# One more FFN pair by seven block products, with GpSimd taking part of the sums of x

## The chip, the cores and the metric

The kernel runs on one core of a Trainium2 chip. The metric is the device time of one execution in microseconds (us), the median of several runs. TensorE (PE in the profile) multiplies; VectorE (DVE), ScalarE (ACT) and GpSimd (POOL) work on tiles in SBUF; SyncE (SP) issues most DMAs and GpSimd some.

## The reference

One inference step of a 4-layer decoder for 512 prompt tokens and 8 sample tokens (520 columns), model width 1024, in float32. Each layer has a mixer (pooling, convolution, differential attention, pooling) and then an FFN, and it is the FFN that the change touches:

```python
def swiglu(h, w_gate, w_up, w_down):
    return (jax.nn.silu(h @ w_gate) * (h @ w_up)) @ w_down
...
    xp = xp + swiglu(rmsnorm(xp, norm_ffn[i]), ffn_w_gate[i], ffn_w_up[i], ffn_w_down[i])
```

D_FF is 2816, that is 22 tiles of 128 rows for gate and 22 for up.

## The kernel before

Activations lie transposed: 8 tiles of 128 channels by 520 tokens, taken by TensorE in two halves of 260. Every float32 value is split into a high part and a low part (ScalarE writes the high part, rounded to fp32r; VectorE subtracts it from the value and writes the low part), and each product is made of three matmuls: high by high, high by low, low by high.

A gate tile and its up tile are a **pair**; an FFN has 22. An **ordinary pair** is two **units** of 8 x 2 x 3 = 48 matmuls, 96 in all: `unit` on the un-normed x, and `rstd` multiplies the result (`gate_n`, `up2`). `h2` is up2 by silu2. Four pairs of a layer are ordinary (PLAIN = 4): units 0 to 7. The other 18 are **pairs in sevens**: gate and up tile by two halves of the channels form a 2 by 2 product with the two halves of the tokens, done in seven block products (Winograd's form of Strassen) of 4 x 3 = 12 matmuls, 84 in all. They run in `seven_blocks` on TensorE and `join` on ScalarE and VectorE; b counts the blocks 0 to 6.

The sevens need x otherwise than the units do. VectorE makes the normed halves xn0 and xn1 (16 `scaled` instructions of 260 columns, in the first ordinary pair), then four sums of them, `xt[:, 0]`, `xt[:, 1]`, `xt3` and `xt[:, 2]` (1040 columns each), and for each block b the high part (ScalarE, `x_high(b)`, into `xn_hi`, `xt_hi`, `late_hi`) and the low part (VectorE, `x_low(b)`). They are placed by hand between the instructions of the ordinary pairs; c counts these. Weights of a pair in sevens need sums too: two on VectorE (`w_sum_2`, `w_sum_4`) and two by accumulating DMAs that GpSimd issues (`weight_sums`); the second of them adds to a half of w_up that SyncE loads into `w_sum` after a wait for the sums of x.

Each engine runs its own program in order, and semaphores tie them. The ones of the change are `x_scaled`, `x_summed`, `xs_hi_ok`, `xs_lo_ok`. TensorE's `unit` n waits for `split_lo` (VectorE's low part of the weights, `w_lo`), block b for `blk_lo` and `xs_lo_ok`; blocks 2, 4 and 6 add to what block 0 left in PSUM, and wait until ScalarE has copied it (`copy_begun`, tile `begun`, semaphore `begun_ok`).

## Time and profile before

| | |
|---|---|
| median of 3 runs | 2039.98 us (2039.18 to 2043.82) |
| the profiled execution | 2047.97 us, its span 2046.2 us |
| busy share of the span | TensorE 98%, VectorE 66%, ScalarE 52%, GpSimd 19% |
| granted TensorE clock, mean | 0.991 |
| layer 0's ordinary pairs | 53.5 to 101.5 us |

The profile is one execution. Its times are from the span's start. In a timeline a row gives start, duration, engine, line, operation, output from inputs with shapes, and in brackets how long the engine was idle ahead of it and who ended that.

### The profile page before, as it was taken

The numbers are of one execution on the slowest core, as the hardware profiler recorded it, in microseconds if no ns is written. First come the engines' busy times: TensorE is split into PE (matmuls) and PEld (weight loads), VectorE is DVE, ScalarE is ACT, GpSimd is POOL, SyncE is SP. The second block draws the span as 40 slices with busy tenths as digits, with TensorE's granted clock in tenths as the row PEclk, the third lists the DMA queues.
The fourth block names the chain that finished last, engine by engine and source line by source line (L and its number), as shares of the span: only waits on it lengthen the run. The fifth ranks groups of instructions, "written<-read, shape, count | busy, mean of one in ns | idle before, by whom it ended". The sixth has DMA issues, their size and how long they took to land.

```text
span 2046.2 us, 41692 instructions
## 1 busy us (share of the span) xinstructions
PE 2006.8 (98%) x16576; PEld 1941.2 (95%) x16576; DVE 1345.7 (66%) x2268; ACT 1061.5 (52%) x1842; POOL 380.8 (19%) x397
## 2 busy tenths in 40 slices
PE   8999999999899999999999979999999999999999
PEld 7999999998599999999999859999999999999998
DVE  4994586468768945864466655885587368936852
ACT  4563465365455634653777753463365355624642
POOL 3210110169421101101111114110111120101101
PEclk8999999999999999999999999999999999999999
DMA  5363664244214636643432252363564314636642
GB/s 188 106 181 91 163 182 128 81 126 115 78 63 113 182 93 165 181 129 88 175 112 88 86 194 92 113 175 97 150 187 138 109 57 127 172 93 182 180 118 80
DMA packets 99526, 264.86 MB, mean 129 GB/s; under 512 B 13353, under 2 KB 16329, under 8 KB 99316
## 3 DMA queue, kind: packets, MB, share of 16 engines
q1 hardware_dynamic: 74756, 217.14, 32.9%
q0 software_dynamic: 24208, 44.72, 11.9%
q8 instruction: 121, 1.98, 0.4%
q10 hardware_dynamic: 384, 0.55, 0.1%
q14 instruction: 57, 0.47, 0.1%
HBM read 213.40 MB, written 8.60 MB: 108 GB/s over the span
## 4 chain that ended last, share of the span: by engine, by line
PE 87%; POOL 4%; DVE 4%; ACT 2%; issue 1%; DMA 1%; SPq 0%; ACTq 0%; POOLq 0%; DVEq 0%
PE acc L693 44%; PE pair L893 20%; PE acc L893 10%; PE bank L893 5%; POOL conv L2600 4%; PE pair L1095 1%; PE pair L774 1%; PE bank L1115 1%; DMA hist_rows<-in_state_pool 1%; DVE w_lo L1858 1%; PE pair L1070 1%; DVE xn L1999 1%; DVE xt L2066 0%; ACT w_hi L1328 0%; PE bank L1105 0%
## 5 line engine op out<-in xcount | busy, mean ns | idle before, releaser
L1328 ACT ACTIVATE w_hi<-raw 128x768 fp32r<-128x768 f32 (+1 forms) x220 | 199.3, 906 | 429.9 <-PE acc L693 427.6
L693 PE MATMUL acc<-h_hi,w_hi 128*128 128x260 f32 x1408 | 399.5, 284 | 0.0
L693 PE MATMUL acc<-h_lo,w_hi 128*128 128x260 f32 x1408 | 398.3, 283 | 0.0
L693 PE MATMUL acc<-h_hi,w_lo 128*128 128x260 f32 x1408 | 397.6, 282 | 0.0
L1858 DVE TENSOR_TENSOR w_lo<-raw,w_hi 128x768 fp32r<-128x768 f32 (+1 forms) x220 | 240.9, 1095 | 216.4 <-ACT w_hi L1328 211.0
L693 PE MATMUL acc<-xin_hi,w_hi 128*128 128x260 f32 x1152 | 332.6, 289 | 6.0 <-DVE w_lo L1858 4.8
L693 PE MATMUL acc<-xin_hi,w_lo 128*128 128x260 f32 x1152 | 326.2, 283 | 0.0
L693 PE MATMUL acc<-xin_lo,w_hi 128*128 128x260 f32 x1152 | 325.6, 283 | 0.0
L693 PEld LDWEIGHTS acc<-h_hi,w_hi 128*128 128x128 f32 x1408 | 265.2, 188 | 0.6
L693 PEld LDWEIGHTS acc<-h_hi,w_lo 128*128 128x128 f32 x1408 | 265.1, 188 | 0.0
L693 PEld LDWEIGHTS acc<-h_lo,w_hi 128*128 128x128 f32 x1408 | 264.8, 188 | 0.0
L693 PEld LDWEIGHTS acc<-xin_hi,w_hi 128*128 128x128 f32 x1152 | 217.5, 189 | 20.5 <-issue 13.9
L2537 POOL DMA_DIRECT2D raw<-raw x72 | 62.1, 862 | 922.4 <-DMA raw<-in_ffn_w_up 922.4
L693 PEld LDWEIGHTS acc<-xin_lo,w_hi 128*128 128x128 f32 x1152 | 217.6, 189 | 0.2
L693 PEld LDWEIGHTS acc<-xin_hi,w_lo 128*128 128x128 f32 x1152 | 217.5, 189 | 0.0
L1489 ACT ACTIVATE begun<-pair 128x260 f32<-128x260 f32 x216 | 83.7, 388 | 174.5 <-PE pair L893 174.3
L2034 DVE TENSOR_TENSOR block<-raw,block 128x512 fp32r<-128x512 f32 x140 | 95.7, 686 | 52.7 <-ACT block L1475 52.7
L893 PE MATMUL pair<-xn_hi,block 128*128 128x260 f32 x576 | 114.8, 281 | 0.0
L2503 POOL TENSOR_TENSOR sqacc<-sqacc,sq 128x520 f32<-128x520 f32 x48 | 75.5, 1574 | 208.4 <-ACT sq L1334 207.9
L893 PE MATMUL pair<-xt_hi,block 128*128 128x260 f32 x544 | 109.5, 284 | 0.0
L893 PE MATMUL bank<-xn_hi,block 128*128 128x260 f32 x544 | 109.2, 282 | 0.0
L1475 ACT ACTIVATE w_hi<-w_sum 128x512 fp32r<-128x512 f32 x144 | 90.2, 627 | 29.9 <-PE acc L893 12.9
(442 smaller groups left out, 5377.8 us busy)
## 6 DMA issues: line engine op xcount, KB each, us to landing
raw<-in_ffn_w_gate SPq DMA_DIRECT2D x88, 512.0 KB, 3.6
raw<-in_ffn_w_up SPq DMA_DIRECT2D x88, 512.0 KB, 4.5
raw<-in_ffn_w_down SPq DMA_DIRECT2D x64, 384.0 KB, 3.2
raw<-in_ffn_w_down SPq DMA_DIRECT2D x64, 320.0 KB, 2.9
w_sum<-in_ffn_w_up SPq DMA_DIRECT2D x72, 256.0 KB, 4.8
raw<-raw POOLq DMA_DIRECT2D x72, 256.0 KB, 3.4
w_sum<-raw POOLq DMA_DIRECT2D x72, 256.0 KB, 4.1
raw<-in_attn_w_qkv SPq DMA_DIRECT2D x24, 512.0 KB, 3.6
```

The lines of the kernel that those rows point to most:

```text
L693: last = pe.matmul(acc[:, b, 0:HALF], w[:, w_tile * P:(w_tile + 1) * P], v[:, h * HALF:(h + 1) * HALF], start=start and t == 0, stop=stop ...
L774: last = pe.matmul(pair[:, m % 2, b * P:(b + 1) * P], x_tok[:, b, cols], band_s[:, b, g, 0:P], start=True, stop=b == 0)
L893: last = pe.matmul(block_bank(J, b), w[:, cols], v[:, k, :], start=k + t == 0 and b in (0, 1, 3, 5), stop=k == 3 and t == 2, skip_group_ch ...
L1070: last = pe.matmul(pair[:, t, 0:HALF], blk, sq[:, 0, t * HALF:(t + 1) * HALF], start=True, stop=True)
L1328: act.activation(w_hi[n.slot(2)][:, 0:cols], raw[:, q.slot(4), 0:cols], ACT.Copy).then_inc(split_hi, 1)
L1475: act.activation(block_w(j, b)[0], block_of(b, q, J), ACT.Copy).then_inc(blk_hi, 1)
L1489: act.activation(begun[b // 2][:], pair[:, J % 2, 0:HALF], ACT.Copy).then_inc(begun_ok, 1)
L1858: dve.tensor_tensor(w_lo[n.slot(2)][:, 0:cols], raw[:, raw_of(n).slot(4), 0:cols], w_hi[n.slot(2)][:, 0:cols].bitcast(F32), ALU.subtract). ...
L2034: dve.tensor_tensor(lo, block_of(b, raw_of_pair(layer, j), PAIRS * layer + j), hi.bitcast(F32), ALU.subtract).then_inc(blk_lo, 1)
L2503: pool_e.tensor_tensor(sqacc[:], sqacc[:], sq[:, m % 2, :], ALU.add).then_inc(sq_added, 1)
L2537: pool_e.dma_start(up[:, 0:512], up[:, 512:1024], accum_op=ALU.add).then_inc(ups_ok[J % 2], 16)
L2600: pool_e.tensor_tensor(out, out, prod_p[:, p % 3, :], ALU.add).then_inc(prod_added, 1)
```

## The change

PLAIN goes from 4 to 3: each layer has three ordinary pairs (units 0 to 5) and nineteen in sevens. So the work on x has to be placed in three pairs. Two sums (`xt[:, 2]`, `xt3`) and the low parts of blocks 4 and 6 go from VectorE to GpSimd, with a semaphore `x_by_pool`. VectorE's remaining work on x stands in two places of the second ordinary pair: two sums and the low part of block 0 ahead of up2, the low parts of blocks 1 to 3 at its end; that of block 5 stays in the last.

```diff
-PLAIN = 4
+PLAIN = 3
...
-                            sp.wait_ge(x_summed, 4 * layer + 4)
+                            sp.wait_ge(x_summed, 2 * layer + 2)
...
-                    pe.wait_ge(xs_lo_ok, 7 * layer + b + 1)
+                    if b in XP_LOW:
+                        pe.wait_ge(x_by_pool, 4 * layer + XP_LOW[b])
+                    else:
+                        pe.wait_ge(xs_lo_ok, 5 * layer + min(b, 4) + 1)
...
                     if c == 1:
                         dve.wait_ge(x_scaled, layer + 1)
                         dve.wait_ge(stored, 16 * STORED[("pool0", "conv", "attn", "pool1")[layer]])
-                        for to, a, b, made in ((xt[:, 0], xn1[:, 0:4], xn0[:, 0:4], 0), (xt[:, 1], xn1[:, 4:8], xt[:, 0], 1),
-                                         (xt3[:], xn0[:, 4:8], xt[:, 1], 2), (xt[:, 2], xn1[:, 0:4], xn1[:, 4:8], 0)):
...
-                    if c + 2 == PLAIN:
-                        x_low(1)
-                        x_low(2)
+                        x_sum(0)
+                        x_sum(1)
+                        x_low(0)
...
                     if c + 1 == PLAIN:
                         low(0, 4)
-                        x_low(4)
-                        for b in (5, 6):
-                            x_low(b)
-                            low(0, b)
+                        x_low(5)
+                        low(0, 5)
+                        low(0, 6)
...
-                    if c + 3 == PLAIN:
-                        x_low(0)
                     if c + 2 == PLAIN:
-                        x_low(3)
+                        for b in range(1, 4):
+                            x_low(b)
...
+            def sums(layer):
+
+                pool_e.wait_ge(x_scaled, layer + 1)
+                pool_e.tensor_tensor(xt[:, 2], xn1[:, 0:4], xn1[:, 4:8], ALU.subtract).then_inc(x_by_pool, 1)
+                up_sum(layer, 0)
+                pool_e.wait_ge(x_summed, 2 * layer + 2)
+                pool_e.tensor_tensor(xt3[:], xn0[:, 4:8], xt[:, 1], ALU.subtract).then_inc(x_by_pool, 1)
+                crossed_sum(layer, 0)
+                up_sum(layer, 1)
+                crossed_sum(layer, 1)
+                x_low(layer, 4)
+                x_low(layer, 6)
+                for j in range(2, PAIRS):
+                    up_sum(layer, j)
+                    crossed_sum(layer, j)
```

ScalarE's code is the same but for its waits, and since its places are counted from PLAIN it moves too. In layer 0 ScalarE's rows from the first ordinary pair's second weight split on were, before:

```order
L1328 ACTIVATE w_hi1_58<-raw_56 128x1024
L1480 ACTIVATE h_hi_77<-h2_102 128x520
L1328 ACTIVATE w_hi0_57<-raw_56 128x1024
L1499 ACTIVATE silu2_99<-gate_n_100 128x520
L1328 ACTIVATE w_hi1_58<-raw_56 128x1024
L1480 ACTIVATE h_hi_77<-h2_102 128x520
L1460 ACTIVATE xn0_hi_80<-xn0_79 128x1040
```

and in the change:

```order
L1335 ACTIVATE w_hi1_58<-raw_56 128x1024
L1489 ACTIVATE h_hi_77<-h2_102 128x520
L1469 ACTIVATE xn0_hi_80<-xn0_79 128x1040
L1335 ACTIVATE w_hi0_57<-raw_56 128x1024
L1508 ACTIVATE silu2_99<-gate_n_100 128x520
L1469 ACTIVATE xn0_hi_80<-xn0_79 128x1040
L1469 ACTIVATE xt_hi_82<-xt_81 128x1040
L1335 ACTIVATE w_hi1_58<-raw_56 128x1024
```

The high part of block 0's x (`x_high(0)`, the first xn0_hi) moved from the end of the second ordinary pair to the end of the first, ahead of the split for unit 4 (w_hi0). VectorE's rows of layer 0 from the second ordinary pair's gate_n on were, before:

```order
L2050 TENSOR_TENSOR gate_n_100<-acc,rstd_52 128x520
L1858 TENSOR_TENSOR w_lo0_59<-raw_56,w_hi0_57 128x1024
L2066 TENSOR_TENSOR xt_81<-xn1_88,xn0_79 128x1040
L2066 TENSOR_TENSOR xt_81<-xn1_88,xt_81 128x1040
L2066 TENSOR_TENSOR xt3_89<-xn0_79,xt_81 128x1040
L2066 TENSOR_TENSOR xt_81<-xn1_88 128x1040
L2071 TENSOR_TENSOR up2_101<-acc,rstd_52 128x520
L2080 TENSOR_TENSOR h2_102<-up2_101,silu2_99 128x520
L1858 TENSOR_TENSOR w_lo1_60<-raw_56,w_hi1_58 128x1024
L2040 TENSOR_TENSOR h_lo_78<-h2_102,h_hi_77 128x520
```

and in the change:

```order
L2068 TENSOR_TENSOR gate_n_100<-acc,rstd_52 128x520
L1867 TENSOR_TENSOR w_lo0_59<-raw_56,w_hi0_57 128x1024
L2015 TENSOR_TENSOR xt_81<-xn1_88,xn0_79 128x1040
L2015 TENSOR_TENSOR xt_81<-xn1_88,xt_81 128x1040
L2029 SCALAR_TENSOR_TENSOR xn0_lo_84<-xn0_79,xn0_hi_80 128x1040
L2084 TENSOR_TENSOR up2_101<-acc,rstd_52 128x520
L2092 TENSOR_TENSOR h2_102<-up2_101,silu2_99 128x520
L1867 TENSOR_TENSOR w_lo1_60<-raw_56,w_hi1_58 128x1024
L2058 TENSOR_TENSOR h_lo_78<-h2_102,h_hi_77 128x520
L2027 TENSOR_TENSOR xn0_lo_84<-xn0_79,xn0_hi_80 128x1040
L2027 TENSOR_TENSOR xt_lo_85<-xt_81,xt_hi_82 128x1040 x2
L2038 TENSOR_TENSOR w_sum_94<-raw_56 128x512
```

Two of the four sums left this place and block 0's low part came ahead of up2; three low parts follow h_lo, where an ordinary pair's gate_n stood before. GpSimd's queue in layer 0, which held only the accumulating DMAs here, begins in the change with

```order
L2565 TENSOR_TENSOR xt_81<-xn1_88 128x1040
L2547 DMA raw_56<-raw_56 128x512
L2568 TENSOR_TENSOR xt3_89<-xn0_79,xt_81 128x1040
L2554 DMA w_sum_94<-raw_56 128x512
L2547 DMA raw_56<-raw_56 128x512
L2554 DMA w_sum_94<-raw_56 128x512
L2560 TENSOR_TENSOR xt_lo_85<-xt_81,xt_hi_82 128x1040
L2560 TENSOR_TENSOR late_lo_91<-xt3_89,late_hi_90 128x1040
```

Four computing instructions of 1040 columns stand among the DMAs of the first two pairs in sevens.

## Rows read from the trace of the kernel before

**Rows 1.** The page, part 1: busy time, share of the span, instructions of each engine.
```profile
PE 2006.8 (98%) x16576; PEld 1941.2 (95%) x16576; DVE 1345.7 (66%) x2268; ACT 1061.5 (52%) x1842; POOL 380.8 (19%) x397
```
**Rows 2.** The chain in order of time, layer 0: start, duration, what.
```profile
110.33 2.88 PE pair L893 x24
120.40 2.88 PE pair L893 x24
```
**Rows 3.** Timeline of TensorE, layer 0: the first matmul of unit 5.
```profile
84.16 0.39 PE L693 MATMUL acc<-xin_hi,w_hi 128*128 128x260 f32 x1 [0.78 <-DVE w_lo L1858]
```
**Rows 4.** Timeline of ScalarE, layer 1: weight splits released by a unit's end.
```profile
634.51 1.06 ACT L1328 ACTIVATE w_hi<-raw 128x1024 fp32r<-128x1024 f32 x1 [3.54 <-PE acc L693]
640.25 1.06 ACT L1328 ACTIVATE w_hi<-raw 128x1024 fp32r<-128x1024 f32 x1 [3.73 <-PE acc L693]
```
**Rows 5.** Windows: stretch, length; busy us (count) of PE, PEld, DVE, ACT, POOL; clock, DMA.
```profile
53.50:101.70 48.20, 47.39 (x390) 47.00 (x391) 43.95 (x57) 26.81 (x34) 8.40 (x9) 1.00 0.41 112
```
**Rows 6.** Timeline of VectorE, layer 0.
```profile
71.67 3.29 DVE L1999 SCALAR_TENSOR_TENSOR xn<-x,vec,rstd 128x260 f32<-128x260 f32 x8
74.88 0.69 DVE L2050 TENSOR_TENSOR gate_n<-acc,rstd 128x520 f32<-128x520 f32 x1
...
76.62 1.23 DVE L2066 TENSOR_TENSOR xt<-xn,xn 128x1040 f32<-128x1040 f32 x1
...
94.80 0.68 DVE L2020 TENSOR_TENSOR w_sum<-raw 128x512 f32<-128x512 f32 x1
...
96.74 0.68 DVE L2034 TENSOR_TENSOR block<-raw,block 128x512 fp32r<-128x512 f32 x1
```
**Rows 7.** Timeline of ScalarE, layer 0.
```profile
72.01 1.06 ACT L1328 ACTIVATE w_hi<-raw 128x1024 fp32r<-128x1024 f32 x1 [1.32 <-PE acc L693]
...
83.55 1.06 ACT L1460 ACTIVATE xn_hi<-xn 128x1040 fp32r<-128x1040 f32 x1
84.51 1.05 ACT L1328 ACTIVATE w_hi<-raw 128x1024 fp32r<-128x1024 f32 x1
...
96.85 0.64 ACT L1499 ACTIVATE silu<-gate_n 128x520 f32<-128x520 f32 x1 [0.70 <-DVE gate_n L2050]
97.40 0.61 ACT L1475 ACTIVATE w_hi<-raw 128x512 fp32r<-128x512 f32 x1
...
103.15 0.39 ACT L1489 ACTIVATE begun<-pair 128x260 f32<-128x260 f32 x1 [0.37 <-PE pair L893]
```
**Rows 8.** Timeline of VectorE, layer 1.
```profile
635.15 0.69 DVE L2050 TENSOR_TENSOR gate_n<-acc,rstd 128x520 f32<-128x520 f32 x1
```
**Rows 9.** Timelines of VectorE and GpSimd, layer 1; last row from pooling, undisturbed.
```profile
611.42 1.23 DVE L1858 TENSOR_TENSOR w_lo<-raw,w_hi 128x1024 fp32r<-128x1024 f32 x1 [0.39 <-ACT w_hi L1328]
612.57 1.80 DVE L1870 SCALAR_TENSOR_TENSOR xin_lo<-x,vec,xin_hi 128x520 fp32r<-128x520 f32 x1
...
612.00 1.81 POOL L2503 TENSOR_TENSOR sqacc<-sqacc,sq 128x520 f32<-128x520 f32 x1 [3.91 <-ACT sq L1334]
...
1669.30 0.76 DVE L1870 SCALAR_TENSOR_TENSOR xin_lo<-x,vec,xin_hi 128x520 fp32r<-128x520 f32 x1
```
**Rows 10.** The same two engines in the first pooling layer.
```profile
50.71 3.21 POOL L2503 TENSOR_TENSOR sqacc<-sqacc,sq 128x520 f32<-128x520 f32 x2 [2.40 <-ACT sq L1334]
...
52.69 1.41 DVE L1891 SCALAR_TENSOR_TENSOR x<-acc,vec,x 128x520 f32<-128x520 f32 x2
```
**Rows 11.** GpSimd's instructions by line: durations in ns, lowest/median/highest.
```profile
L2654 POOL TENSOR_TENSOR o_tok<-o_tok,o_tmp x8: 1042/1047/1047, 1222.0 to 1231.2; 128x512 f32<-128x512 f32 x8
L2581 POOL TENSOR_TENSOR diag_z<-const,taps_z x4: 1967/1982/2436, 478.4 to 515.7; 128x1024 f32<-128x1024 f32 x4
L2600 POOL TENSOR_TENSOR conv<-conv,prod_p x60: 1261/1296/2284, 428.3 to 535.7; 128x512 f32<-128x512 f32 x60
```
**Rows 12.** The page, part 6: DMA issues, KB each, us from issue to landing.
```profile
w_sum<-in_ffn_w_up SPq DMA_DIRECT2D x72, 256.0 KB, 4.8
...
w_sum<-raw POOLq DMA_DIRECT2D x72, 256.0 KB, 4.1
```

More of the change, by code:

```diff
@@ L480, in trunk_step @@
         xs_hi_ok, xs_lo_ok = sem("xs_hi_ok"), sem("xs_lo_ok")
+        x_by_pool = sem("x_by_pool")
         begun_ok, joined, new_scaled = sem("begun_ok"), sem("joined"), sem("new_scaled")
@@ L1457, in x_high @@
                     if X_SUMMED[b]:
-                        act.wait_ge(x_summed, 4 * layer + X_SUMMED[b])
+                        act.wait_ge(x_summed, 2 * layer + X_SUMMED[b])
+                    if XP_SUMMED[b]:
+                        act.wait_ge(x_by_pool, 4 * layer + XP_SUMMED[b])
                     own, hi, _ = XS[b]
@@ L2000, in scaled, with x_sum @@
                     return last
+                def x_sum(t):
+                    if t:
+                        dve.wait_ge(x_summed, 2 * layer + 1)
+                    dve.tensor_tensor(xt[:, t], xn1[:, 4 * t:4 * t + 4], xt[:, 0] if t else xn0[:, 0:4], ALU.subtract)\
+                       .then_inc(x_summed, 1)
                 def x_low(b):
@@ L2005, in x_low @@
                     if X_READ[b]:
-                        dve.wait_ge(x_summed, 4 * layer + X_READ[b])
+                        dve.wait_ge(x_summed, 2 * layer + X_READ[b])
+                    if XP_READ[b]:
+                        dve.wait_ge(x_by_pool, 4 * layer + XP_READ[b])
                     own, hi, lo = XS[b]
@@ L2529, in store_stage, with up_sum @@
                 pool_e.dma_start(states_s, stage[hist:hist + DEC, :]).then_inc(stored, 16)
-            def weight_sums(layer):
-                for j in range(PAIRS):
-                    q, J = raw_of_pair(layer, j), PAIRS * layer + j
-                    gate, up = raw[:, q.slot(4), :], raw[:, (q + 1).slot(4), :]
-                    pool_e.wait_ge(landed[(q + 1).slot(4)], ((q + 1).turn(4).v + 1) * 16)
-                    pool_e.dma_start(up[:, 0:512], up[:, 512:1024], accum_op=ALU.add).then_inc(ups_ok[J % 2], 16)
-                    pool_e.wait_ge(landed[q.slot(4)], (q.turn(4).v + 1) * 16)
-                    pool_e.wait_ge(crossed_in[J % 2], 16 * (J // 2 + 1))
-                    pool_e.dma_start(crossed(J), gate[:, 0:512], accum_op=ALU.add).then_inc(crossed_ok[J % 2], 16)
+            def up_sum(layer, j):
+                q, J = raw_of_pair(layer, j), PAIRS * layer + j
+                up = raw[:, (q + 1).slot(4), :]
+                pool_e.wait_ge(landed[(q + 1).slot(4)], ((q + 1).turn(4).v + 1) * 16)
+                pool_e.dma_start(up[:, 0:512], up[:, 512:1024], accum_op=ALU.add).then_inc(ups_ok[J % 2], 16)
@@ new lines, in crossed_sum, with x_low @@
+            def crossed_sum(layer, j):
+                q, J = raw_of_pair(layer, j), PAIRS * layer + j
+                pool_e.wait_ge(landed[q.slot(4)], (q.turn(4).v + 1) * 16)
+                pool_e.wait_ge(crossed_in[J % 2], 16 * (J // 2 + 1))
+                pool_e.dma_start(crossed(J), raw[:, q.slot(4), 0:512], accum_op=ALU.add).then_inc(crossed_ok[J % 2], 16)
+            def x_low(layer, b):
+                pool_e.wait_ge(xs_hi_ok, 7 * layer + b + 1)
+                own, hi, lo = XS[b]
+                pool_e.tensor_tensor(lo, own, hi.bitcast(F32), ALU.subtract).then_inc(x_by_pool, 1)
@@ L2573, in _ @@
                     state_rows(0)
-                weight_sums(3 * q)
+                sums(3 * q)
                 if q:
@@ L2608, in _ @@
                 add_squares(3)
-                weight_sums(1)
+                sums(1)
                 add_squares(4)
@@ L2661, in _ @@
                 add_squares(5)
-                weight_sums(2)
+                sums(2)
                 add_squares(6)
```

10 lines of the change are left out of this document (5 added, 5 removed).

## The prediction, written before the changed kernel was run

> **What bounds the kernel now.** The page's first part comes first: TensorE is busy 98% of the span, VectorE 66%, GpSimd 19% [rows 1]. The chain of work in order of time then shows what an FFN costs. Pieces of one block repeat every 10.07 us, one period per pair in sevens [rows 2], and a pair has 7 blocks of 12 matmuls, so a matmul costs 10.07 / 84 = 0.12 us. An ordinary pair is two units of 48; ScalarE's splits, each released by the end of a unit, stand 5.74 us apart [rows 4], again 0.12 us a matmul. So TensorE is never late in an FFN, except once each in layers 0 and 3, before unit 5 (of units 0 to 7): its last matmul of unit 4 ended 0.78 us before 84.16 [rows 3]; a matmul's record ends 0.28 after its start, so unit 5 was due at 84.16 - 0.78 - 0.28 + 0.12 = 83.2, and with a slow second matmul the wait costs about 1.0 us. Unit 4 began at 83.2 - 5.74 = 77.5. Whatever takes matmuls away there is worth their time; whatever makes TensorE wait costs the wait in full.
>
> What limits the ordinary pairs is how full VectorE is. In layer 0 it is busy 43.95 of the 48.2 us before the first block [rows 5]. The timeline of VectorE shows it back to back: each instruction starts about 0.09 us before the one ahead ends [rows 6].
>
> **The change, part by part.**
>
> *Fewer matmuls.* In each layer one pair goes from 96 matmuls to 84: 12 x 0.12 = 1.44 us, four layers 5.8 us gained. That is the whole gain.
>
> *Less time for the same work on x.* Two units fewer are 11.5 us less before block 0.0 (block b of pair j is j.b). VectorE loses with them one ordinary pair's instructions, and two sums and two low parts of 1.23 us each [rows 6] that go to GpSimd. The rest must now fit. I walk layer 0 instruction by instruction, in the new order, with the durations of the rows, 0.03 us from an engine's end to another's start and 0.12 to TensorE's.
>
> *GpSimd's price.* No GpSimd instruction of before has two full inputs of 1040. The form with one spread input takes 1.05 us at 512 and 1.97 at 1024, so about 0.12 is fixed; two full inputs at 512 take 1.26 when undisturbed [rows 11], hence (1.26 - 0.12) x 1040 / 512 + 0.12 = 2.4 us. Bounds: 2.0 (the one-spread-input form) and 2.54 (twice the whole of 1.26 and a little).
>
> *GpSimd stops VectorE.* The rows at 612 us show it. GpSimd's sum starts at 612.00 while VectorE's w_lo still runs and takes 1.81 us instead of 1.26; VectorE's xin_lo, at 612.57, takes 1.80 instead of 0.76 and ends 0.56 after GpSimd's [rows 9]. Both read two tensors in SBUF. An instruction that reads PSUM and one SBUF tensor isn't stopped: two of them take 1.41 us as usual under a GpSimd pair [rows 10]. I take 2.2 of GpSimd's 2.4 us as lost when VectorE wants the path at once, since xin_lo ended 0.2 earlier than a fresh start would have. The Trainium skill ("SBUF — State Buffer", section "SBUF: two separate sides") calls the shared pair an exclusive lock held for the whole instruction. By that reading all 2.4 us are lost and the sum below is +18.6 instead of +15; the row's 0.56 us speaks for a little less.
>
> *Unit 4 (layer 0).* This is a new wait: ScalarE's first high part of x stands ahead of the split for unit 4 and waits for the last of the scaled parts, which VectorE ends at 71.67 + 3.29 = 74.96 [rows 6]. Before, that split ran at 72.01 [rows 7] and nothing waited for it. Now the high part runs from 75.0 (1.06 us, the next one 0.97 later [rows 7]), the split from 76.0 to 77.1. GpSimd started its first sum at 75.0 and ends at 77.4, so VectorE's w_lo (1.23 [rows 9]) begins effectively at 77.25, ends 78.46, and unit 4 starts at 78.6 instead of 77.5: 1.05 us.
>
> *Unit 5.* VectorE: two sums to 80.9, low part of block 0's x to 82.0, up2 from PSUM to 82.6. GpSimd, released at 80.9, waits for the low part and holds 81.95 to 84.4; h2 reads SBUF and ends at 84.9 instead of 83.4; w_lo ends at 86.0. Unit 5 is due at 84.3: 1.8 us.
>
> *Block 0.0.* Behind it VectorE has h_lo (0.7), three low parts (1.15 each from start to start), two w_sums (0.7 each), gate_n (0.6) and the low part of the block (0.7) [rows 6]: 92.6. TensorE is due at 91.9: 0.85 us.
>
> *Blocks 0.2 and 0.4.* ScalarE's silu comes after gate_n, then two w_hi (0.53 each from start to start), two high parts (0.97 each) and the copy begun [rows 7]. Before, ScalarE did the first of them while TensorE was still at the last unit; now gate_n itself is late (ends 92.0) and they stand end to end: silu 92.0, w_hi 92.6 and 93.1, high parts 93.65 and 94.6, begun 95.6 to 96.0. Block 0.2 is due at 92.7 + 2 x 1.44 = 95.6: 0.5 us. The second begun, behind two more w_hi, costs block 0.4 another 0.5.
>
> *Blocks 0.5, 0.6, 1.2.* GpSimd's low parts run 94.7 to 97.2 and 97.6 to 100.0 and stop VectorE twice, 2.0 and 2.1 us, where it has w_lo, late_lo and h2 in line. The w_lo of block 0.5 ends at 101.6 (due 101.0): 0.8; h2 at 102.8 holds ScalarE, whose third begun comes at 103.8: 0.75; the same lag reaches pair 1's block 2: 0.5. From pair 2 on the slack of the steady state has absorbed it.
>
> GpSimd's DMAs aren't on the path: the half of w_up is issued at 80.9, lands 4.8 us later, the addition another 4.1 [rows 12], at 89.8; its reader comes at 93.1. SyncE's wait for the sums falls from four to two, so the loads behind it in its queue go out no later than VectorE frees their slots. Behind GpSimd's wait for the last high part stand only pair 2's additions, whose weights land later anyway.
>
> *Sum.* Layers 0 and 3: 1.05 + 1.8 + 0.85 + 0.5 + 0.5 + 0.8 + 0.75 + 0.5 = 6.8 of waiting, less the 1.0 there now, less 1.44: +4.4 us each. In layer 1 gate_n starts at 635.15 [rows 8], and unit 3's end releases ScalarE at 640.25 [rows 4], so unit 4 is due at about 640.05, 4.9 us after gate_n; in layer 0 that is 77.5 - 74.9 = 2.6. Unit 4 then has no wait. From gate_n to unit 5's start the walk took 86.1 - 74.9 = 11.2 us: 646.35, due 645.8, 0.55 us. The rest is the same: 0.55 + 0.85 + 0.5 + 0.5 + 0.8 + 0.75 + 0.5 = 4.5, less 1.44: +3.1 each, in layer 2 too, whose rows repeat layer 1's. Together 2 x 4.4 + 2 x 3.1 = +15 us. The profiled execution of 2047.97 us (span 2046.2) would become 2063; it stands 8 us above the median, and I carry the difference over: 2039.98 + 15 = 2055 us.
>
> With GpSimd's 2.0 us the same walk gives +9; with 2.54 us and the whole of it lost, +20.5. The skill's "GPSIMD Engine Reference" ("Instruction dispatch") gives about 2.5 cycles an element for two inputs. An estimate by that figure and the 1.2 GHz of the "SBUF — State Buffer" page is 2.2 us for 1040, and the sum would be +11; no row here has this shape.
>
> **The rivals.** *VectorE isn't stopped (not slower).* If these instructions don't share the path as those at 612 us did, the same walk leaves, in layer 0, unit 4 0.9, unit 5 0.4, blocks 0.0, 0.2 and 0.4 0.85, 0.5 and 0.5: 3.15 - 1.0 - 1.44 = +0.7; in layer 1 0.86 - 1.44 = -0.6. Together +0.1: no change, 2040. For it: GpSimd is on other tensors. Against it: so it was at 612 us. It decides where a stop is short: with GpSimd instructions of 1.6 us (stops of 1.4) the walk gives +4, with 1.2 us +1, with under 0.9 us +0.1.
>
> *GpSimd is slower than its shape says.* 3.1 us an instruction, twice the disturbed 1.5: the walk gives +26, 2066. The rows at 512 that last 2.28 us [rows 11] contain waiting, which I count already.
>
> *The waits are hidden.* If ScalarE and VectorE keep up after all, the 5.8 us come in full and the two present waits may go: -6 to -8, 2033. Against it: VectorE's 43.95 busy us [rows 5] must fit into 11.5 us less, less what leaves.
>
> **How the numbers follow.** Forecast +15 (with its bounds +9 to +20.5): 0.74. A mixture, where only some of the four instructions stop VectorE, +5 to +9 (the two sums alone give +7 in the walk): 0.07. GpSimd at 3.1: 0.07. Not stopped: 0.08. Hidden: 0.04. A measurement of this kernel can tell about 0.2%, 4 us, from no change, so slower has 0.74 + 0.07 + 0.07 = 0.88, within 0.08, faster 0.04. The range takes in forecast and mixture, +5 to +20.5 and 2 us at the top for the step from profile to median: 2045 to 2063; 0.19 is left out.
>
> **What would show it.** VectorE instructions with two SBUF inputs of about 2.9 to 3.4 us instead of 0.7 to 1.2 beside GpSimd's four, two per place; GpSimd's xt at 2.4 to 3.5 us. TensorE's first wait on w_lo at unit 4 in layers 0 and 3 alone, a longer one at unit 5 in all four, then waits in pair 0 on w_lo and begun; pairs from 2 on at 10.07 us. Eight pairs in sevens before the first down stage. The walk is wrong if VectorE's instructions beside GpSimd's keep their length, if TensorE waits for GpSimd itself, or if later pairs are slower as well.

## The result, and the profile after

The changed kernel takes 2055.57 us (median of six runs, 2052.31 to 2061.46); the kernel before, timed beside it, 2041.38 us. The ratio is 1.0062 with a 95% interval of 1.0047 to 1.0077: 12.7 us slower, between 9.6 and 15.7. Forecast were 15 us.

In all comparisons below a change of time is the ratio less one, times 2041 us.

The page of the profile, part 1 (busy time, share of the span, instructions) and the first line of part 4 (shares of the chain that ended last) of the changed kernel:

```profile
PE 1999.5 (97%) x16528; PEld 1928.1 (94%) x16528; DVE 1365.3 (66%) x2292; ACT 1072.9 (52%) x1878; POOL 430.4 (21%) x421
...
PE 79%; DVE 7%; issue 4%; ACT 4%; POOL 4%; DMA 1%; ACTq 0%; SPq 0%; DVEq 0%; POOLq 0%
```

TensorE has 48 matmuls and 7.3 us less to do than in [rows 1], and a longer span. VectorE has 19.6 us *more* busy time, although four instructions a layer went to GpSimd. Two things make this up. A pair in sevens gives VectorE more to do than an ordinary pair: with all four pieces left on VectorE (the first experiment below) it is busy 1359.9 us, 14.2 more than before. And a stopped instruction counts as busy: the sixteen pieces that left are some 20 us of work (1.23 us each), and VectorE is busy 5.4 us more than in that experiment, not 20 less. GpSimd is busy 49.6 us more.

The timeline of TensorE, layer 0 (start, duration, what; idle time before it and what ended it), all the waits after the first unit:

```profile
69.60 0.38 PE L697 MATMUL acc<-xin_hi,w_hi 128*128 128x260 f32 x1 [0.99 <-DVE w_lo L1867]
...
77.17 0.39 PE L697 MATMUL acc<-xin_hi,w_hi 128*128 128x260 f32 x1 [1.55 <-DVE w_lo L1867]
...
83.77 0.39 PE L900 MATMUL pair<-xn_hi,block 128*128 128x260 f32 x1 [0.59 <-DVE block L2052]
...
87.08 0.39 PE L900 MATMUL pair<-xt_hi,early 128*128 128x260 f32 x1 [0.15 <-ACT begun L1498]
...
90.39 0.39 PE L900 MATMUL pair<-xt_hi,w_hi 128*128 128x260 f32 x1 [0.15 <-ACT begun L1498]
...
92.88 0.39 PE L900 MATMUL acc<-late_hi,w_hi 128*128 128x260 f32 x1 [0.79 <-DVE w_lo L2052]
...
95.04 0.38 PE L900 MATMUL pair<-late_hi,w_hi 128*128 128x260 f32 x1 [0.47 <-ACT begun L1498]
...
99.99 0.39 PE L900 MATMUL pair<-xt_hi,block 128*128 128x260 f32 x1 [0.37 <-ACT begun L1498]
```

In place of the one row of [rows 3] there are eight: units 4 and 5, then blocks 0.0, 0.2, 0.4, 0.5, 0.6 and 1.2, and no other. The idle times in brackets add up to 5.06 us. Each leaves out what a restart costs beside it (the prediction counted 1.0 us for a bracket of 0.78), and with 0.22 us for each of the eight the sum is 6.8.

The clean measure is the length of the stage from the first matmul of the feed-forward to the first of the down projection. Here it is for each layer, in us (read from the timeline of TensorE and the chain in order of time):

| layer | before | after | difference | forecast |
|---|---|---|---|---|
| 0 | 53.53 to 172.21: 118.68 | 44.51 to 167.90: 123.39 | +4.7 | +4.4 |
| 1 | 615.81 to 733.79: 117.98 | 611.53 to 732.95: 121.42 | +3.4 | +3.1 |
| 2 | 1288.01 to 1405.85: 117.84 | 1286.21 to 1407.60: 121.39 | +3.6 | +3.1 |
| 3 | 1680.62 to 1799.18: 118.56 | 1683.91 to 1807.24: 123.33 | +4.8 | +4.4 |

Together +16.5 us. The two profiled spans differ only by 8.3 (2054.5 and 2046.2), since the profiled execution of before came to its first feed-forward 9 us later. The windows from 20 to 36 us show why, before and then after (length; busy us and count of PE, PEld, DVE, ACT, POOL; granted clock; DMA):

```profile
20.00:36.00 16.00, 16.00 (x72) 14.92 (x71) 5.87 (x13) 3.29 (x6) 0.00 (x0) 0.51 0.47 180
20.00:36.00 16.00, 16.00 (x142) 15.96 (x141) 10.39 (x20) 8.36 (x15) 2.56 (x3) 1.00 0.50 194
```

TensorE did 72 matmuls there at a granted clock of 0.51, nearly all at 1.2 GHz, and 142 at 1.00, that is 2.4 GHz. The first feed-forward began between 44.5 and 53.8 us in the thirteen profiles of this study, whose kernels do the same up to there: by 45.8 us in the five in which the clock stayed at 1.00, after 51.6 us in the six in which it was low for over 13 us. So the stages are compared and not the spans.

Who makes TensorE wait is seen on VectorE and GpSimd, whose timelines of layer 0 go side by side:

```profile
66.00 2.46 POOL L2565 TENSOR_TENSOR xt<-xn 128x1040 f32<-128x1040 f32 x1 [10.99 <-DVE xn L2008]
...
72.06 3.36 POOL L2568 TENSOR_TENSOR xt<-xn,xt 128x1040 f32<-128x1040 f32 x1 [2.75 <-DVE xt L2015]
...
85.88 2.42 POOL L2560 TENSOR_TENSOR xt_lo<-xt,xt_hi 128x1040 fp32r<-128x1040 f32 x1 [2.79 <-ACT xt_hi L1469]
88.59 2.54 POOL L2560 TENSOR_TENSOR late_lo<-xt,late_hi 128x1040 fp32r<-128x1040 f32 x1 [0.29 <-ACT late_hi L1469]
```
```profile
68.01 1.53 DVE L1867 TENSOR_TENSOR w_lo<-raw,w_hi 128x1024 fp32r<-128x1024 f32 x1 [1.48 <-ACT w_hi L1335]
69.47 1.23 DVE L2015 TENSOR_TENSOR xt<-xn,xn 128x1040 f32<-128x1040 f32 x1
...
71.89 1.23 DVE L2029 SCALAR_TENSOR_TENSOR xn_lo<-xn,xn_hi 128x1040 fp32r<-128x1040 f32 x1
73.04 0.69 DVE L2084 TENSOR_TENSOR up<-acc,rstd 128x520 f32<-128x520 f32 x1
73.84 2.13 DVE L2092 TENSOR_TENSOR h<-up,silu 128x520 f32<-128x520 f32 x1
...
86.05 2.80 DVE L2052 TENSOR_TENSOR w_lo<-w_sum,w_hi 128x512 fp32r<-128x512 f32 x1
88.77 3.46 DVE L2027 TENSOR_TENSOR late_lo<-xn,late_hi 128x1040 fp32r<-128x1040 f32 x1
92.15 0.68 DVE L2052 TENSOR_TENSOR w_lo<-w_sum,w_hi 128x512 fp32r<-128x512 f32 x1
```

Four instructions of VectorE are long, each beside one of GpSimd: w_lo 1.53 us (1.22 elsewhere), h 2.13 (0.70), w_lo 2.80 (0.68), late_lo 3.46 (1.23). GpSimd waits too: its second sum takes 3.36 us, since VectorE's low part (71.89 to 73.12) stands in the way. The two engines take turns. The instruction at 73.04, which reads PSUM and one tensor in SBUF, keeps its 0.69 us beside GpSimd's.

### The profile page after: what moved, and what is told of

Same layout as the page of the kernel before. It is cut to its first block, busy times and chain, and to the rows that moved or that the text cites. A ratio compares the mean times of both kernels' runs of the same rounds, so it can differ in the third digit from the quotient of the medians.

```text
span 2054.5 us, 41744 instructions
## 1 busy us (share of the span) xinstructions
PE 1999.5 (97%) x16528; PEld 1928.1 (94%) x16528; DVE 1365.3 (66%) x2292; ACT 1072.9 (52%) x1878; POOL 430.4 (21%) x421
## 4 chain that ended last, share of the span: by engine, by line
PE 79%; DVE 7%; issue 4%; ACT 4%; POOL 4%; DMA 1%; ACTq 0%; SPq 0%; DVEq 0%; POOLq 0%
PE acc L697 37%; PE pair L900 20%; PE acc L900 10%; PE bank L900 5%; POOL conv L2636 4%; DVE xn L2008 1%; PE pair L1102 1%; ACT w_hi L1335 1%; DVE w_lo L1867 1%; PE bank L1122 1%; PE pair L1077 1%; DMA hist_rows<-in_state_pool 1%; DVE xt_lo L2027 0%; PE pair L778 0%; PE pair L1272 0%
## 5 line engine op out<-in xcount | busy, mean ns | idle before, releaser
L1335 ACT ACTIVATE w_hi<-raw 128x768 fp32r<-128x768 f32 (+1 forms) x212 | 190.8, 900 | 400.2 <-PE acc L697 397.7
L1867 DVE TENSOR_TENSOR w_lo<-raw,w_hi 128x768 fp32r<-128x768 f32 (+1 forms) x212 | 232.3, 1096 | 221.7 <-ACT w_hi L1335 216.2
L697 PE MATMUL acc<-xin_hi,w_hi 128*128 128x260 f32 x1024 | 296.0, 289 | 10.7 <-DVE w_lo L1867 9.5
L697 PE MATMUL acc<-xin_hi,w_lo 128*128 128x260 f32 x1024 | 289.3, 282 | 0.0
L697 PE MATMUL acc<-xin_lo,w_hi 128*128 128x260 f32 x1024 | 289.0, 282 | 0.0
L697 PEld LDWEIGHTS acc<-xin_hi,w_hi 128*128 128x128 f32 x1024 | 192.6, 188 | 26.0 <-issue 13.8
L697 PEld LDWEIGHTS acc<-xin_lo,w_hi 128*128 128x128 f32 x1024 | 192.8, 188 | 0.2
L697 PEld LDWEIGHTS acc<-xin_hi,w_lo 128*128 128x128 f32 x1024 | 192.8, 188 | 0.0
L900 PE MATMUL pair<-xn_hi,block 128*128 128x260 f32 x608 | 121.6, 282 | 2.4 <-DVE block L2052 2.4
L2052 DVE TENSOR_TENSOR w_lo<-w_sum,w_hi 128x512 fp32r<-128x512 f32 x152 | 112.6, 741 | 2.0 <-ACT w_hi L1484 1.3
```

Source lines behind the costliest of these rows:

```text
L697: last = pe.matmul(acc[:, b, 0:HALF], w[:, w_tile * P:(w_tile + 1) * P], v[:, h * HALF:(h + 1) * HALF], start=start and t == 0, stop=stop ...
L900: last = pe.matmul(block_bank(J, b), w[:, cols], v[:, k, :], start=k + t == 0 and b in (0, 1, 3, 5), stop=k == 3 and t == 2, skip_group_ch ...
L1335: act.activation(w_hi[n.slot(2)][:, 0:cols], raw[:, q.slot(4), 0:cols], ACT.Copy).then_inc(split_hi, 1)
L1867: dve.tensor_tensor(w_lo[n.slot(2)][:, 0:cols], raw[:, raw_of(n).slot(4), 0:cols], w_hi[n.slot(2)][:, 0:cols].bitcast(F32), ALU.subtract). ...
L2052: dve.tensor_tensor(lo, block_of(b, raw_of_pair(layer, j), PAIRS * layer + j), hi.bitcast(F32), ALU.subtract).then_inc(blk_lo, 1)
```

## The experiments

The theory: an instruction of GpSimd that reads two operands from SBUF stops VectorE's work on two operands in SBUF for as long as it runs, and this, with the shorter front, makes the waits. The rival: nothing is stopped, and only the number and the order of VectorE's own instructions count. Every "walk" in what follows is the prediction's hand calculation, done for another order of the same instructions with the same durations.

### All four pieces back on VectorE

```diff
-        X_SUMMED = (0, 0, 2, 1, 0, 0, 0)
-        XP_SUMMED = (0, 0, 0, 0, 1, 0, 2)
+        X_SUMMED = (0, 0, 2, 1, 4, 0, 3)
...
                         x_sum(1)
+                        x_sum(2)
+                        x_sum(3)
                         x_low(0)
...
                         low(0, 4)
-                        x_low(5)
-                        low(0, 5)
-                        low(0, 6)
+                        x_low(4)
+                        for b in (5, 6):
+                            x_low(b)
+                            low(0, b)
...
-                pool_e.wait_ge(x_scaled, layer + 1)
-                pool_e.tensor_tensor(xt[:, 2], xn1[:, 0:4], xn1[:, 4:8], ALU.subtract).then_inc(x_by_pool, 1)
...
```

> Three ordinary pairs as in the changed kernel, but all four pieces (two sums, two low parts) are back on VectorE, so that GpSimd computes nothing in these stretches. The theory under test (a GpSimd instruction of 2.4 us stops VectorE's three-operand work for 2.2 us of it) and its rival (it stops nothing, only number and place of VectorE's own instructions count) both give this kernel the same time, since there is nothing to stop: walked step by step with the durations of the traces, +10 us against the kernel before. What they differ in is whether the changed kernel (+15) lies above it. In layers 0 and 3 the walk has waits of 0.9 us in TensorE before unit 4, 2.8 before unit 5, 0.85, 0.5 and 0.55 before blocks 0.0, 0.2 and 0.4, and hardly any before blocks 0.5, 0.6 and 1.2, which in the changed kernel have 0.5 to 0.8 each. If the rival holds, this kernel is slower than the changed one (which has 4 pieces less on VectorE) by about 10 us; by the theory it is faster by about 5.

Measured: ratio 1.0065 (1.0043 to 1.0087), +13.3 us; the stages are 122.05, 120.04, 120.06 and 122.18 us long, together 11.3 more than before, where the changed kernel has 16.5. In layer 1 the bracketed waits are 1.26 before unit 5, 0.58, 0.15 and 0.15 before blocks 0.0, 0.2 and 0.4, and no row with a wait later, as walked. So with four instructions a layer *more* on VectorE the kernel isn't slower than the changed one (+13.3 against +12.7 us): the rival's 10 us on top are refuted. That it is 5 us faster is read from the stages alone; the timed runs show no difference.

Most of the loss, then, is there without GpSimd: three ordinary pairs are too short for VectorE's front in this order. Layers 0 and 3 have one more thing in them, though, that the walk didn't have. The windows of this kernel in layer 0 (columns as above):

```profile
76.00:79.00 3.00, 0.63 (x6) 0.42 (x4) 2.90 (x4) 0.98 (x2) 0.00 (x0) 1.00 0.82 244
79.00:82.00 3.00, 2.82 (x13) 2.82 (x14) 3.00 (x5) 1.66 (x3) 0.87 (x1) 0.56 0.63 126
82.00:85.00 3.00, 3.00 (x24) 3.00 (x23) 2.96 (x5) 0.64 (x1) 1.46 (x2) 0.87 0.98 253
```

After the wait of 2.55 us before unit 5 the granted clock is 0.56, then 0.87: some of the time ran at 1.2 instead of 2.4 GHz, 13 matmuls in 3 us instead of 25. While TensorE was slow VectorE caught up, and the waits before 0.0, 0.2 and 0.4 are missing in this layer. Layer 3 does the same: 0.56 in the 3 us from 1714 on, behind a wait of 2.54 us. The lengths came out near the walk's (+3.4 and +3.6, where its terms give +3.2) because one replaced the other, which the walk had not foreseen.

### Only the low parts back, only the sums back

The first has the changed kernel's sums on GpSimd and the diff above for x_low alone; the second the reverse.

> The changed kernel with its two low parts back on VectorE; the two sums stay on GpSimd. By the theory (the second pair of GpSimd instructions costs more in stopped VectorE time than it saves): the waits before blocks 0.5 and 0.6 go, that before 1.2 shrinks to 0.1, units 4 and 5 keep theirs (1.05 and 1.8 in layers 0 and 3): +7 us against the kernel before, 8 faster than the changed kernel. By the rival (nothing is stopped) it would be at +0.5, and the changed kernel at +0.1.

> The changed kernel with its two sums back on VectorE; the two low parts stay on GpSimd. By the theory: units 4 and 5 wait 0.9 and 2.8 us in layers 0 and 3, unit 5 1.4 in layers 1 and 2, blocks 0.5, 0.6 and 1.2 keep 0.5 to 0.8: +18 us against the kernel before, above the changed kernel. By the rival: +10, and the blocks 0.5 and 0.6 do not wait.

Measured: 1.0033 (1.0018 to 1.0047), +6.7 us, with the low parts back; 1.0086 (1.0059 to 1.0112), +17.6 us, with the sums back. The stages add +8.2 and +19.3 us. TensorE's timeline in layer 1 of the version with the low parts back, from unit 5 on:

```profile
647.67 0.39 PE L696 MATMUL acc<-xin_hi,w_hi 128*128 128x260 f32 x1 [0.57 <-DVE w_lo L1863]
...
654.27 0.39 PE L896 MATMUL pair<-xn_hi,block 128*128 128x260 f32 x1 [0.59 <-DVE block L2048]
...
657.58 0.39 PE L896 MATMUL pair<-xt_hi,early 128*128 128x260 f32 x1 [0.16 <-ACT begun L1494]
```

No row has a wait at 0.5, 0.6 or 1.2. In the version with the sums back it is the other way round: 1.26 us before unit 5, and 0.85, 0.42 and 0.36 before blocks 0.5, 0.6 and 1.2. So the two pairs of GpSimd instructions are separate, and have opposite signs: the sums on GpSimd save 3 us by the stages (11.3 to 8.2), since they shorten the crowded place before unit 5; the low parts on GpSimd cost 8 us (8.2 to 16.5 with the sums there, 11.3 to 19.3 without), since VectorE is stopped for 2.1 and 2.2 us to save it twice 1.15. Without them the kernel is at +6.7 instead of +12.7 us. This is the largest single part of the loss that is GpSimd's.

### Four ordinary pairs, the four pieces on GpSimd

```diff
-PLAIN = 3
+PLAIN = 4
...
-                        x_low(0)
+                    if c + 2 == PLAIN:
+                        x_low(1)
+                        x_low(2)
...
+                    if c + 3 == PLAIN:
+                        x_low(0)
                     if c + 2 == PLAIN:
-                        for b in range(1, 4):
-                            x_low(b)
+                        x_low(3)
```

> The kernel before (four ordinary pairs, VectorE's work on x in its three places), with only the four pieces moved to GpSimd at the points where the changed kernel has them. By the theory: one wait of 1.05 us before unit 4 and one of 0.6 before unit 7 in layers 0 and 3, then 0.4, 0.75 and 0.5 before blocks 0.5, 0.6 and 1.2 (0.5 before 0.6 and 1.2 in layers 1 and 2): +6.5 us against the kernel before. By the rival VectorE is only relieved: -2 us, since the kernel before's own wait before unit 5 goes too.

Measured: 1.0038 (1.0022 to 1.0055), +7.8 us, where the theory had +6.5 and the rival -2. In layer 0 the brackets are 0.97 before unit 4, 0.23, 0.43 and 0.37 before blocks 0.5, 0.6 and 1.2; that before unit 7 has no row. The stages add +7.2 us. GpSimd's help costs time also where the number of ordinary pairs stays.

### Extra work for GpSimd that nobody needs

In the kernel before, nothing is moved; GpSimd gets one of three things at each of the four points, with the result in a scratch tensor.

```diff
+            def extra():
+
+                if made[0]:
+                    pool_e.wait_ge(extra_done, made[0])
+                pool_e.tensor_tensor(sq[:].rearrange("p a b -> p (a b)"), const[:, 0:2 * T], const[:, 8:2 * T + 8], ALU.subtract).then_inc(extra_done, 1)
+                made[0] += 1
...
             def weight_sums(layer):
 
+                pool_e.wait_ge(x_scaled, layer + 1)
+                extra()
                 for j in range(PAIRS):
...
+                    if j == 0:
+                        pool_e.wait_ge(x_summed, 4 * layer + 2)
+                        extra()
...
+                    if j == 1:
+                        for b in (4, 6):
+                            pool_e.wait_ge(xs_hi_ok, 7 * layer + b + 1)
+                            extra()
```

In the second and third the subtraction is replaced by two tensor_copy (128x1040 and 128x520) and by three memset. ScalarE's squares of the next pooling, which use the same scratch, wait for it; that lies outside the stages.

> The kernel before, in which nothing of VectorE's or ScalarE's work is moved; only GpSimd gets something to do that nobody needs: one subtraction of 128x1040 (two operands read from SBUF, the result written into the scratch of squares, free at that time) at each of the four points at which the changed kernel gives it a sum or a low part. The output is the reference's. Nobody waits for these results in the front of the feed-forward, only GpSimd's own weight sums stand behind them. By the theory that a two-operand instruction of GpSimd stops VectorE: +16 us against the kernel before, by waits in layers 0 and 3 of 1.05 before unit 4, 1.6 before unit 5, 0.5, 1.9 and 0.5 before blocks 0.5, 0.6 and 1.2, and the same without unit 4 and with 0.4 before unit 5 in layers 1 and 2; VectorE's instructions beside them last 2.8 us and more where they lasted 0.7 and 1.23. By the rival (the moved pieces' own order and waits cost the time, not the use of the memory by GpSimd): within 1 us of the kernel before.

> As the run with four extra two-operand subtractions, but at each of the four points GpSimd makes two copies (one operand read, one written) of 128x1040 and 128x520. The output is the reference's. If any GpSimd instruction of that length stops VectorE, the time is as there, about +16 us; if only instructions with two operands do, it is within 1 us of the kernel before, and VectorE's instructions beside them keep their 0.7 and 1.23 us. I hold the second for likelier, since the kernel's own copies on GpSimd stand in stretches in which nothing can be read on this.

> As the run with four extra two-operand subtractions, but with three memsets (nothing read, 128x1040 twice and 128x520 written) at each of the four points, about 2.4 us of GpSimd's time as well. The output is the reference's. If it is GpSimd's writing or its mere presence that stops VectorE, the time is about +16 us; if it is the reading of operands, it is within 1 us of the kernel before.

Measured: subtractions 1.0113 (1.0091 to 1.0135), +23.1 us; copies 1.0047 (1.0029 to 1.0065), +9.6 us; memsets 1.0004 (0.9989 to 1.0019), +0.8 us. The stages add +22.8, +8.2 and +0.2 us. What each did to VectorE's low part of split 4, in the same place of layer 0 (GpSimd's row, then VectorE's; subtraction, copy, memset):

```profile
66.59 2.46 POOL L2540 TENSOR_TENSOR sq<-const 128x1040 f32<-128x1040 f32 x1 [10.99 <-DVE xn L2002]
...
67.04 3.10 DVE L1861 TENSOR_TENSOR w_lo<-raw,w_hi 128x1024 fp32r<-128x1024 f32 x1
```
```profile
75.32 1.05 POOL L2540 COPY sq<-const 128x1040 f32<-128x1040 f32 x1 [10.96 <-DVE xn L2002]
76.44 1.50 POOL L2544 COPY sq<-const 128x520 f32<-128x520 f32 x1
...
75.78 1.67 DVE L1861 TENSOR_TENSOR w_lo<-raw,w_hi 128x1024 fp32r<-128x1024 f32 x1
77.38 1.65 DVE L2069 TENSOR_TENSOR xt<-xn,xn 128x1040 f32<-128x1040 f32 x1
```
```profile
67.02 0.97 POOL L2540 MEMSET sq<- 128x1040 f32 x1 [10.96 <-DVE xn L2002]
...
67.49 1.22 DVE L1861 TENSOR_TENSOR w_lo<-raw,w_hi 128x1024 fp32r<-128x1024 f32 x1
```

The copies show the turns one by one: the first ends at 76.37, and w_lo, begun at 75.78, ends 1.08 us later, at 77.45; only then does the second copy run, for its half microsecond, and ends at 77.94 after 1.50; and the sum that VectorE began at 77.38 ends 1.09 us after that. Beside the memset w_lo keeps its 1.22 us. So it is GpSimd's *reading* of SBUF that stops VectorE, with one operand as with two, until GpSimd's instruction ends. The Trainium skill has this rule ("SBUF — State Buffer", section "Who interferes with whom"): a VectorE instruction with two SBUF inputs contends with a GpSimd instruction that reads SBUF, not with one that only writes it. These three runs agree with it.

Of my expectations one mechanism and one size were wrong. The theory spoke of two operands, and I had held it for likelier that copies stop nothing; they do. They cost less than the subtractions, and they are shorter: a copy of 128x1040 takes 1.05 us and one of 520 about 0.5, 1.6 a place against 2.46; a walk with stops of that length, done afterwards, gives +6. And the subtractions cost 23 us, not 16. Here the walk was short at the third and fourth: the bracket before block 0.5 is 1.43 us in layer 0 and 1.27 in layer 1, where it had 0.5, for the fourth subtraction got its turn one instruction of VectorE earlier than walked, so that the low part of late_hi and that of block 0.5 both stood behind it. In layers 0 and 2 one more stop is longer than the turns explain, and TensorE then waits before unit 7 too (0.33 and 0.39 us), for which the walk had no term. In layer 0:

```profile
81.42 0.93 POOL L2551 DMA_DIRECT2D raw<-raw  x1 [12.37 <-DMA raw<-in_ffn_w_up]
82.06 2.77 POOL L2540 TENSOR_TENSOR sq<-const 128x1040 f32<-128x1040 f32 x1
...
81.59 4.35 DVE L2012 TENSOR_TENSOR xn_lo<-xn,xn_hi 128x1040 fp32r<-128x1040 f32 x1 [0.53 <-ACT xn_hi L1463]
```

VectorE's instruction began 0.47 us before GpSimd's by the records and still ended 1.1 us after it (4.38 us in layer 2, begun 0.51 ahead). In layers 1 and 3 it began 0.57 and 0.69 us ahead and kept its 1.24. The copies show it in all four layers at this place, with VectorE 0.30 to 0.42 us ahead; in layer 0:

```profile
89.68 1.40 POOL L2540 COPY sq<-const 128x1040 f32<-128x1040 f32 x1
...
89.33 2.85 DVE L2012 TENSOR_TENSOR xn_lo<-xn,xn_hi 128x1040 fp32r<-128x1040 f32 x1 [0.54 <-ACT xn_hi L1463]
```

At the fourth place, where GpSimd was idle before, a lead of 0.1 us was enough for VectorE's low part (99.04 against 99.14) to keep its 1.23 us. Here GpSimd's instruction stands directly behind its own DMA issue, and its record begins before that of the issue ends (82.06 against 82.35) and is longer (2.77 against 2.46), so its start may not be what the record says. In the run with memsets VectorE's same instruction lies beside the same DMA issue and takes 1.24 us, so the issue alone isn't it. Why GpSimd comes first there stays open.

### ScalarE's x_high(0) behind split 4

```diff
                     if c + 2 == PLAIN:
+                        x_high(0)
                         x_high(1)
...
-                    if c + 3 == PLAIN:
-                        x_high(0)
```

> The changed kernel with one instruction moved on ScalarE: x_high(0) stands behind split 4 and the second silu instead of ahead of split 4. The prediction laid the 1.05 us before unit 4 of layers 0 and 3 to this x_high(0), which waits for VectorE's last scaled column and holds split 4. The walk now says otherwise: GpSimd's first sum starts at the same moment (the last scaled column) and stops VectorE's low part of split 4 for as long, so that unit 4 waits 1.05 us with x_high(0) moved too, and the time stays at the changed kernel's (+15 us against the kernel before). If the prediction's reading is right, the 1.05 us go in layers 0 and 3 and the time is 2 us lower.

> Three ordinary pairs with all four pieces on VectorE (as in the first experiment, measured at +13 us by its timed runs and +11 by its stage lengths), and x_high(0) on ScalarE behind split 4 and the second silu. Here GpSimd stops nothing, and what delays split 4 is x_high(0) alone: the walk has the wait before unit 4 (0.9 in layers 0 and 3) go, that before unit 5 fall from 2.8 to 2.1 in layers 0 and 3 and from 1.4 to nothing in layers 1 and 2, and the time fall by 6 us to +4 (by the stage lengths +5). If x_high(0) has no part in it, nothing changes.

Measured, in the changed kernel: 1.0068 (1.0051 to 1.0085), +13.9 us; the bracket before unit 4 is 0.97 us (0.99 in the changed kernel), and layer 0's stage is 123.39 us long, to the hundredth as before the move. GpSimd's first sum and VectorE's low part of split 4, which now begins early and is stopped:

```profile
73.31 2.44 POOL L2564 TENSOR_TENSOR xt<-xn 128x1040 f32<-128x1040 f32 x1 [10.97 <-DVE xn L2007]
...
73.75 3.07 DVE L1866 TENSOR_TENSOR w_lo<-raw,w_hi 128x1024 fp32r<-128x1024 f32 x1
```

In the version with all on VectorE: 1.0034 (1.0021 to 1.0046), +6.9 us; the stages add 4.8 us instead of 11.3, and the wait before unit 4 has gone. Both readings of unit 4's wait were therefore half right: x_high(0) does hold split 4, but in the changed kernel GpSimd's first sum holds VectorE until the same moment, and taking one away gains nothing. With all on VectorE the moved x_high(0) is worth 6.5 us by the stages, more than the two sums and nearly as much as the two low parts, because VectorE is then also earlier at unit 5: the waits there are 1.91 us instead of 2.55 in layer 0, and gone in layers 1 and 2.

### Can three ordinary pairs pay?

VectorE's front in another order, everything on VectorE, x_high(0) behind split 4; the edit is shown against the version just before (all on VectorE, x_high(0) moved):

```diff
                     if c + 1 == PLAIN:
                         w_sum_2(0)
-                        w_sum_4(0)
...
-                    if c + 1 < PLAIN:
-                        split(n + 2)
-                    else:
-                        for b in range(4):
-                            low(0, b)
...
                         x_sum(0)
+                    if c + 1 < PLAIN:
+                        split(n + 2)
+                    else:
+                        w_sum_4(0)
+                        for b in range(4):
+                            low(0, b)
+                    if c == 0:
+                        for k in range(4, KT):
+                            last = scaled(k)
+                        last.then_inc(x_scaled, 1)
+                    if c == 1:
                         x_sum(1)
-                        x_sum(2)
                         x_sum(3)
                         x_low(0)
...
+                    if c == 1:
+                        x_sum(2)
                     dve.wait_ge(sg_ready, f + 1)
...
-                    if c == 0:
-                        for k in range(4, KT):
-                            last = scaled(k)
-                        last.then_inc(x_scaled, 1)
```

> Three ordinary pairs, everything on VectorE, x_high(0) behind split 4, and VectorE's front in another order: the first scaled half ahead of split 2's low part and the second before up 0, the first sum ahead of split 4's low part, the third sum behind up 1, the second weight sum of pair 0 behind the last gate. The walk has one wait of 2.2 us before unit 2 in layers 0 and 3 (in place of those before units 4 and 5), 0.5 before block 0.4, and hardly any other, in all -0.1 us against the kernel before: the third ordinary pair's removal gives back its 5.8 us and no more. The rival (with three ordinary pairs VectorE's load is simply too large for the front in any order): at least +4, as the version with only x_high(0) moved.

Measured: 1.0007 (0.9993 to 1.0021), +1.4 us; the stages add +2.1, -0.3, -0.3 and +1.7 us, together 3.2. Order alone brings three ordinary pairs from +13.3 us to a difference that the timed runs can't tell from nothing. In layers 1 and 2, which have no wait before unit 2, VectorE's load fits, and the rival is refuted there. For the whole it isn't clearly: 3.2 us by the stages lie under its +4, but the timed interval reaches 4.3. Layers 0 and 3 are longer than walked: a wait of 2.2 and one of 0.5 us, less the 1.0 that goes and the 1.44 of the matmuls, would be +0.3 each. Layer 0's windows:

```profile
60.00:66.00 6.00, 4.28 (x36) 4.08 (x35) 5.60 (x11) 5.23 (x7) 1.05 (x2) 1.00 0.30 93
66.00:72.00 6.00, 5.67 (x34) 5.67 (x35) 5.90 (x13) 0.64 (x1) 0.00 (x0) 0.72 0.30 87
72.00:78.00 6.00, 6.00 (x52) 6.00 (x51) 4.73 (x7) 3.51 (x4) 0.93 (x1) 1.00 0.45 116
```

Its wait of 2.04 us before unit 2 is followed by a granted clock of 0.72 and only one later wait, 0.37 us before block 1.2. In layer 3 the same wait of 2.04 us is followed by a clock of 1.00 and instead by a wait of 1.02 before block 0.2, at which layer 0 has none. So layer 0 loses at the low clock about what layer 3 loses by waiting, and at the full clock it would, by layer 3, not have kept to the walk either.

### One sum of the kernel before, later

```diff
-                                         (xt3[:], xn0[:, 4:8], xt[:, 1], 2), (xt[:, 2], xn1[:, 0:4], xn1[:, 4:8], 0)):
+                                         (xt3[:], xn0[:, 4:8], xt[:, 1], 2)):
...
                         split(n + 3)
+                        if c == 1:
+                            dve.tensor_tensor(xt[:, 2], xn1[:, 0:4], xn1[:, 4:8], ALU.subtract).then_inc(x_summed, 1)
```

> The kernel before with one instruction moved on VectorE: the last of the four sums of x stands behind the low part of split 5 instead of with the three others. Nothing else differs. The walk has the kernel before wait once in its front, 1.06 us before unit 5 in layers 0 and 3 (its trace shows that wait), since four sums stand between split 4 and split 5; with the sum behind split 5 no wait is left, and the time falls by 2.1 us (0.1%), too little for the timed runs to tell from no change but to be seen in the trace as a missing wait. The rival: the sum is then late for its readers (the x_high that needs it, the transfer that waits for all four sums), and a wait comes up later, before block 0.4 or 1.2.

Measured: 2038.44 us against 2042.96, ratio 0.9987 (0.9974 to 1.0001), -2.7 us. The interval still touches 1, but in the trace the wait of [rows 3] is gone from layer 0 and nothing has come in its place in pair 0 or 1, and the stages add -1.8 us, where the walk had -2.1. It has the lowest median of the study, four ordinary pairs and nothing on GpSimd.

## Why the prediction was right

**The sum.** +15 us forecast, +12.7 (9.6 to 15.7) timed, +16.5 by the stages. Each layer came out 0.3 to 0.5 us above its term. The stages of the one profiled pair lie 0.8 us above the timed interval, and no run here says why; an execution can lose 9 us to the low clock ahead of the first feed-forward, so medians of six are rough at this size.

**Fewer matmuls, 5.8 us gained.** Seen best in layer 1 of the reordered version: waits of 0.39 and 0.15 in brackets, with 0.22 for each restart 1.0 us, in a stage that is 0.3 us shorter than before; so about 1.3 of the 1.44 us are there. The period of 10.07 us from pair 2 on is unchanged:

```profile
106.01 2.88 PE pair L900 x24
...
116.08 2.88 PE pair L900 x24
```

These are two pieces of the chain in order of time of the changed kernel, as in [rows 2].

**GpSimd's price, 2.4 us.** The means of the four are 2.42, 2.45, 2.56 and 3.37 us, the last with 0.9 us of waiting in it. The estimate from the 512-column rows held; the prediction's other one, 2.2 us from cycles an element, was too low.

**2.2 of 2.4 us lost.** VectorE lost 0.3 (w_lo, begun when GpSimd had 0.45 us left), 1.43, 2.12 and 2.23 us. The exclusive hold for the whole instruction, which the prediction set against the row at 612 us, is what the traces show: each stopped instruction of 1.23 us ends about 1.1 us after GpSimd's, in the copies twice, and each of 0.68 us ends 0.55 after. So VectorE loses what is left of GpSimd's instruction less about 0.13 us, where I took off 0.2. That this much of its work is done before it needs the path is how I read it; no run separates it.

**Where TensorE waits.** All eight places of layer 0 and all seven of layer 1 were named, and no others came. Brackets against terms in layer 0: unit 4 0.99 (1.05), unit 5 1.55 (1.8), block 0.0 0.59 (0.85), 0.2 and 0.4 0.15 each (0.5), 0.5 0.79 (0.8), 0.6 0.47 (0.75), 1.2 0.37 (0.5). With 0.22 us for each restart the sum is 6.8, as forecast.

**Its causes.** One was misread: unit 4's wait was laid to ScalarE's x_high(0) ahead of the split. The move of x_high(0) alone changed nothing; GpSimd's first sum, which the same paragraph also reckons with, would have held the unit as long. The term was right in size, not in its single cause.

**What the prediction didn't separate.** By the stages the 16.5 us are +11.3 for three ordinary pairs with all of it on VectorE, -3 for the sums on GpSimd and +8 for the low parts on GpSimd; and of the 11.3, 6.5 hang on x_high(0)'s place on ScalarE. Its term for unit 5 had GpSimd's second sum stop h2, and h2 was stopped (2.13 us instead of 0.70); yet the two sums together took less from VectorE (0.3 and 1.43 us) than they spared it (twice 1.15), and the two low parts took more (2.12 and 2.23). The prediction had each wait, but said nowhere that the low parts were the piece to leave out.

**The rivals.** "VectorE isn't stopped" fell with the extra subtractions (+23 us by work that nobody needs) and with the memsets (nothing). "GpSimd at 3.1 us" fell with the durations. "The waits are hidden" fell with the eight waits; even in another order three ordinary pairs come out at +1.4 us, not at -6 to -8.

## What to carry to other kernels

Before work is moved from VectorE to GpSimd, ask what it reads and what VectorE does meanwhile: a GpSimd instruction of 2.4 us that reads SBUF stopped VectorE's instructions with two inputs in SBUF for up to 2.2 us, to save it 1.15, so on these numbers it pays only where VectorE would be idle, or is at work from PSUM (0.69 us beside GpSimd's as alone); here two sums paid 3 us and two low parts cost 8. Filling (memset), which only writes, stopped nothing. And before a stretch of TensorE's work is shortened, walk the engines that feed it, in order, over the new length: the 5.8 us of saved matmuls were certain, and 22 us of waits took them back, while the order of a few instructions on VectorE and ScalarE was worth 12 us by the timed runs and 8 by the stages.
